# Seven buffers for the retention states, and norm sums on VectorE for three of four heads, in a hybrid decoder layer on one core

## The reference, cut to what matters

```python
# per sample b and head h, S is 256 x 512
o = (q * gamma) @ S + (q @ k) * v           # L = 1: scores, state read
S_new = gamma * S + outer(k, v)             # new_state_ret_sample
...
omu = jnp.mean(o, -1, keepdims=True)        # over the 512 columns of a head
ovar = jnp.mean(jnp.square(o - omu), -1, keepdims=True)
on = ((o - omu) * lax.rsqrt(ovar + EPS)).reshape(B, T, D_V) * ret_gn_g
y_b = (on * silu(g_ret)) @ w_ret_out
```

## Time and profile before

| | us |
|---|---|
| median of 3 runs | 788.26 |
| lowest and highest run | 786.79, 789.68 |
| the profiled execution | 790.2 |
| its span, first to last instruction | 788.3 |
| TensorE busy in it (share) | 762.3 (97%) |
| VectorE | 667.8 (85%) |
| ScalarE | 512.8 (65%) |
| mean granted clock of TensorE | 0.996 of 2.4 GHz |

### The profile page before, as it was taken

How to read it: one execution, slowest core, us unless ns; L and a number is a source line. 1 busy time by engine, 2 the same in 40 slices (tenths; PEclk the granted TensorE clock), 3 DMA queues, 4 the chain that set the end, 5 groups by cost and what they waited for, 6 DMA issues and landing times.

```text
span 788.3 us, 12126 instructions
## 1 busy us (share of the span) xinstructions
PE 762.3 (97%) x4747; PEld 655.4 (83%) x4747; DVE 667.8 (85%) x903; ACT 512.8 (65%) x641; POOL 97.3 (12%) x120
## 2 busy tenths in 40 slices
PE   9999999999998999999999998999999999999994
PEld 5999999767776789999899975888888888888873
DVE  5699999877877889899977677999888998999897
ACT  7433446566759576335586463788888788887863
POOL 1100000233332300000002001111111111110000
PEclk9999999999999999999999999999999999999998
DMA  9954454699889845454449653999999999999971
GB/s 347 385 170 178 163 189 158 213 322 335 284 291 313 296 161 180 153 197 174 160 160 334 242 214 115 354 361 370 368 379 364 362 358 368 366 367 363 345 286 75
DMA packets 39174, 213.28 MB, mean 271 GB/s; under 512 B 7381, under 2 KB 7637, under 8 KB 19244
## 3 DMA queue, kind: packets, MB, share of 16 engines
q1 hardware_dynamic: 23268, 165.39, 56.6%
q0 software_dynamic: 15408, 45.71, 16.6%
q10 hardware_dynamic: 432, 1.31, 0.4%
HBM read 193.45 MB, written 31.65 MB: 286 GB/s over the span
## 4 chain that ended last, share of the span: by engine, by line
PE 69%; DVE 13%; DMA 9%; ACT 4%; issue 2%; POOL 1%; DVEq 0%; ACTq 0%; POOLq 0%
PE bank L1868 34%; PE bank L1596 26%; DMA out_ret_sample<-S_ring 4%; DVE conv L1142 3%; DVE w_lo L1095 3%; DMA S_ring<-in_state_ret 2%; PE bank L1741 2%; PE bank L1858 2%; DMA raw<-weights 1%; DMA out_ret_sample<-S_five 1%; ACT w_hi L755 1%; PE bank L1898 1%; PE bank L1654 1%; DMA con<-constants 1%; PE bank L1613 1%
## 5 line engine op out<-in xcount | busy, mean ns | idle before, releaser
L1596 PE MATMUL bank<-h_hi,w_hi 128*128 128x264 f32 (+1 forms) x640 | 188.6, 295 | 4.3 <-DVE w_lo L1095 3.3
L1596 PE MATMUL bank<-h_lo,w_hi 128*128 128x264 f32 (+1 forms) x640 | 184.0, 288 | 0.0
L1596 PE MATMUL bank<-h_hi,w_lo 128*128 128x264 f32 (+1 forms) x640 | 184.0, 287 | 0.0
L1100 DVE TENSOR_TENSOR ring_lo<-raw,ring_hi 128x2048 fp32r<-128x2048 f32 x72 | 163.6, 2289 | 23.4 <-ACT ring_hi L762 23.4
L1095 DVE TENSOR_TENSOR w_lo<-raw,w_hi 128x1024 fp32r<-128x1024 f32 x112 | 136.8, 1222 | 32.4 <-ACT w_hi L755 31.9
L755 ACT ACTIVATE w_hi<-raw 128x1024 fp32r<-128x1024 f32 x112 | 117.8, 1052 | 56.4 <-PE bank L1596 52.4
L762 ACT ACTIVATE ring_hi<-raw 128x2048 fp32r<-128x2048 f32 x72 | 138.3, 1921 | 19.7 <-PE bank L1868 19.7
L1596 PEld LDWEIGHTS bank<-h_hi,w_hi 128*128 128x128 f32 x640 | 120.4, 188 | 10.3 <-DVE w_lo L1095 5.0
L1596 PEld LDWEIGHTS bank<-h_lo,w_hi 128*128 128x128 f32 x640 | 120.4, 188 | 0.5 <-issue 0.2
L1596 PEld LDWEIGHTS bank<-h_hi,w_lo 128*128 128x128 f32 x640 | 120.2, 188 | 0.0
L1142 DVE SCALAR_TENSOR_TENSOR conv<-u,vec,conv 128x256 f32<-128x256 f32 x240 | 101.9, 480 | 0.6
(11 more groups left out here) (291 smaller groups left out, 1491.8 us busy)
## 6 DMA issues: line engine op xcount, KB each, us to landing
raw<-weights SPq DMA_DIRECT2D x152, 1024.0 KB, 7.0
S_ring<-in_state_ret POOLq DMA_DIRECT2D x26, 512.0 KB, 7.2
out_ret_sample<-S_ring POOLq DMA_DIRECT2D x26, 512.0 KB, 6.8
S_five<-in_state_ret POOLq DMA_DIRECT2D x6, 512.0 KB, 4.8
out_ret_sample<-S_five POOLq DMA_DIRECT2D x6, 512.0 KB, 7.7
out_ret_prompt<-S_out POOLq DMA_DIRECT2D x8, 256.0 KB, 4.7
y_rows<-xg POOLq DMA_DIRECT2D x4, 512.0 KB, 7.9
raw<-y_rows SPq DMA_DIRECT2D x2, 1024.0 KB, 5.8
```

The lines of the kernel that those rows point to most:

```text
L1100: dve.tensor_tensor(ring_view(ring_lo, k), raw[raw_slot(NCM + k)][:, :].rearrange("p (k n) -> p k n", k=4), ring_view(ring_hi, k).bitcast( ...
L1596: ins = pe.matmul(out, a[:, k, cols], b[:, k0 + k, :], start=first and k == 0 and j == 0, stop=last and k == ks - 1 and j == 2)
```

## The change

There are seven slots. The two new ones (S_more) lie in xT, and xT is loaded behind the last use of them, after the last prompt state's store and before the store of the convolution's last rows. Loads of states 4, 5 and 6 are issued behind rot_ready; later the load of state n + 6 stands where that of n + 4 stood.

For heads 0 to 2 VectorE adds the four blocks of oT to one (two additions, of 528 and 264 columns, in gsq) at the end of steps 6, 10 and 14, and the four blocks of gsq at the end of steps 8, 12 and 16; TensorE multiplies only the one block. Means of heads 0 to 3 are at steps 7, 11, 15, 18 and variances at 9, 13, 17, 19, with the work of all engines that belongs to them. Head 3 keeps its steps and its groups of four.

```diff
-SLOTS = 5
+SLOTS = 7
+GM_AT, GV_AT, GM_SUM, GV_SUM = (7, 11, 15, 18), (9, 13, 17, 19), (6, 10, 14), (8, 12, 16)
...
+        S_more = xT[:, :, :].rearrange("p k n -> p (k n)")[:, 0:4 * DV].rearrange("p (s a e) -> p s a e", s=2, a=2)
...
-            return S_five if n % SLOTS == 4 else S_ring[:, n % SLOTS]
+            i = n % SLOTS
+            return S_ring[:, i] if i < 4 else S_five if i == 4 else S_more[:, i - 5]
...
             for n in range(4):
                 load(n)
-            pool.dma_start(xT[:, :, :], L["tokens_t"]).then_inc(xT_in, 16)
             pool.wait_ge(rot_ready, 8)
-            load(4)
+            for n in range(4, SLOTS):
+                load(n)
...
             store_prompt(NH - 1)
+            for i in (5, 6):
+                pool.wait_ge(S_stored[i], 16 * len(range(i, 32, SLOTS)))
+            pool.wait_ge(S_used, 32)
+            pool.dma_start(xT[:, :, :], L["tokens_t"]).then_inc(xT_in, 16)
...
-            def halved(src):
-
-                n = KT
+            def halved(dst, src, n):
+
                 while n > 1:
                     n //= 2
-                    ins = dve.tensor_tensor(ln_sq[:, 0:n, OUT], src[:, 0:n, OUT], src[:, n:2 * n, OUT], ALU.add)
-                    src = ln_sq
+                    ins = dve.tensor_tensor(dst[:, 0:n, OUT], src[:, 0:n, OUT], src[:, n:2 * n, OUT], ALU.add)
+                    src = dst
                     if n > 1:
                         link(ins)
-                ins.then_inc(csum_ready, 1)
+                return ins
...
+                    if k in GM_SUM:
+                        h = GM_SUM.index(k)
+                        evacuated(dve, ("ot", h))
+                        halved(gsq, oT[:, 4 * h:4 * h + 4, :], 4).then_inc(gsum_ready, 1)
+                    if k in GV_SUM:
+                        dve.wait_ge(osq_ready, GV_SUM.index(k) + 1)
+                        halved(gsq, gsq, 4).then_inc(gsum_ready, 1)
...
-                    if k >= 6 and (k - 6) % 4 == 0 and k <= 18:
-                        h = (k - 6) // 4
-                        evacuated(pe, ("ot", h))
-                        b = opened(("gm", h))
-                        for et in range(4):
-                            ins = pe.matmul(b[:, OUT], cst("mean_v"), oT[:, 4 * h + et, OUT], start=et == 0, stop=et == 3)
-                        done(ins)
...
+                    if k in GM_AT:
+                        h = GM_AT.index(k)
+                        if h < NH - 1:
+                            pe.wait_ge(gsum_ready, 2 * h + 1)
+                            b = opened(("gm", h))
+                            done(pe.matmul(b[:, OUT], cst("mean_v"), gsq[:, 0, OUT], start=True, stop=True))
+                        else:
+                            evacuated(pe, ("ot", h))
+                            b = opened(("gm", h))
+                            for et in range(4):
+                                ins = pe.matmul(b[:, OUT], cst("mean_v"), oT[:, 4 * h + et, OUT], start=et == 0, stop=et == 3)
+                            done(ins)
```

More of the change, by code:

```diff
@@ L255, in _tiles @@
                 add((("ot", (k - 5) // 4), "A"))
-            if k >= 6 and (k - 6) % 4 == 0 and k <= 18:
-                add((("gm", (k - 6) // 4), "D"))
-            if k >= 7 and (k - 7) % 4 == 0 and k <= 19:
-                add((("gv", (k - 7) // 4), "A"))
+            if k in GM_AT:
+                add((("gm", GM_AT.index(k)), "D"))
+            if k in GV_AT:
+                add((("gv", GV_AT.index(k)), "A"))
             if k in (20, 21):
@@ L934, in _ @@
                         act.activation(gsq[:, :, OUT], oT[:, 4 * h:4 * h + 4, OUT], ACT.Square).then_inc(osq_ready, 1)
-                    if k >= 7 and (k - 7) % 4 == 0 and k <= 19:
-                        h = (k - 7) // 4
+                    if k in GV_AT:
+                        h = GV_AT.index(k)
                         seen(act, ("gv", h))
@@ L1764, in _ @@
                         done(ins)
-                    if k >= 6 and (k - 6) % 4 == 0 and k <= 18:
-                        h = (k - 6) // 4
-                        evacuated(pe, ("ot", h))
-                        b = opened(("gm", h))
-                        for et in range(4):
-                            ins = pe.matmul(b[:, OUT], cst("mean_v"), oT[:, 4 * h + et, OUT], start=et == 0, stop=et == 3)
-                        done(ins)
[L1772 to L1776, removed]
-                            ins = pe.matmul(b[:, OUT], cst("mean_v"), gsq[:, et, OUT], start=et == 0, stop=et == 3)
-                        done(ins)
+                    if k in GM_AT:
+                        h = GM_AT.index(k)
+                        if h < NH - 1:
[8 more added lines that the diff above has]
+                            done(ins)
+                    if k in GV_AT:
+                        h = GV_AT.index(k)
+                        if h < NH - 1:
+                            pe.wait_ge(gsum_ready, 2 * h + 2)
+                            b = opened(("gv", h))
+                            done(pe.matmul(b[:, OUT], cst("mean_v"), gsq[:, 0, OUT], start=True, stop=True))
+                        else:
+                            pe.wait_ge(osq_ready, h + 1)
+                            b = opened(("gv", h))
+                            for et in range(4):
+                                ins = pe.matmul(b[:, OUT], cst("mean_v"), gsq[:, et, OUT], start=et == 0, stop=et == 3)
+                            done(ins)
                     if k in (20, 21):
```

6 lines of the change are left out of this document (3 added, 3 removed).

## The result

| | before | after |
|---|---|---|
| median of 7 runs | 789.39 (786.79 to 790.66) | 793.88 (791.12 to 795.65) |
| profiled execution: time, span, mean granted clock | 790.2, 788.3, 0.996 | 793.88, 792.1, 0.987 |

The ratio is 1.0052 (95% interval 1.0034 to 1.0069): the change makes the kernel slower, by about 4.1 us by the ratio (the two medians stand 4.5 apart). The forecast was 788.6, the range ended at 793.0.

The account below looks back on a forecast made before the run. It took TensorE's own work plus 4.5 us of idle as the bound; 8.0 + 4.2 = 12.2 off and 12.5 of new idle on gave +0.3 on 788.26, so 788.6 us, with a range of 780.5 to 793.0.

Parts of the forecast that it names:

- Part 1: Mean and variance products of heads 0 to 2 on TensorE: six four-part products become one-part, 8.0 us off.
- Parts 2 and 3: VectorE's added sums (6.9 us of work) and the later mean and variance steps: together 12.5 us of new TensorE idle.
- The chains: Queues of VectorE and ScalarE work followed through steps 8 to 19, giving 12.5 us of new TensorE idle.
- part 4: Seven state slots instead of five: ScalarE's waits for state loads vanish where they cost, 4.2 us off, bounds 0 and 4.5.
- Slower by the loads: Rival: more loads in flight each land later, ScalarE still waits in steps 11 and 15; 793 us, chance 0.20.
- The full gain: Rival: the new lags do not form, 776.1 us; chance 0.35 together with its half form at 782.4.
- The longer table switch: Rival: ScalarE held 1.3 us more behind each of three table loads, steps 9, 13, 17; 792.5 us, chance 0.01.
- Late sums: Rival: one-part products wait for additions held up by ot's copy, steps 6, 10, 14; 3 us on, 791.6, chance 0.06.

Follow-up runs that it names:

- early21: The changed kernel with means, variances and sums of heads 0 to 2 one step earlier and head 3's variance at step 21: 783.36 us (0.9925).
- shift_only: The kernel before with seven slots and the later mean and variance steps, all still in four products, no sums on VectorE: 790.78 us (1.0021).
- delay: The kernel before with seven slots, plus five unread VectorE reductions ahead of v_two in step 12: 793.7 us in a single execution.
- filled: The changed kernel with three unread 512-column products ahead of TensorE's waits in each of steps 12 and 19: 792.72 us (1.0035).
- filled_all: The changed kernel with unread 512-column products ahead of TensorE's waits in steps 11, 12, 15, 17 and 19: 791.72 us (1.0026).
- after_again: The changed kernel with nothing altered, profiled a second time: 793.2 us.
- slots7: The kernel before with only the seven slots and the later xT load, the norm as before: 787.3 us (0.9964).
- early: The changed kernel with sums one step earlier, so means of heads 0 to 2 at their old steps and their variances one later than before: 785.09 us (0.9927).
- conv_moved: The changed kernel without VectorE's convolution steps in steps 10, 11 and 14, made up for later: 797.26 us (1.0094).
- norm_only: The changed kernel with five slots and xT fetched at the start again: 800.05 us (1.0121).

## Why the prediction was wrong

- **Part 1 held.** One-part products made a step 1.34 (a product gone and one in its place) or 1.69 (gone) shorter: 6.92 to 5.58 in step 6 of early21, 6.92 to 5.22 in step 6 of after. 8.0 in all.
- **Parts 2 and 3 held in their mechanism; that the sum agrees is luck.** The chains gave 12.5 of new idle and the table has 12.5, but the steps miss by +0.3, -0.6, +0.4, -0.8 and +0.4, the 0.3 of steps 10, 14 and 18 were not forecast, and 0.3 of step 19 is clock. The largest error was step 17 (2.7 for 1.9), where the links on ScalarE were sized by likeness. shift_only divides the 12.5: the later steps alone cause 4.0. The other 8.5, more than the 8.0 that the shorter products win, come with the sums and the shorter products together; no run has the one without the other.
- **The first step that failed is a sentence at the start: "The granted clock is 1.00 there ... so clock plays no part."** It is a statement about a kernel with 4.5 of idle time, and the sum put 12.5 in its place. No price was set on idle time beyond its own length. In the profile of after the falls behind steps 12 and 19 cost 1.45 + 1.27 = 2.7. delay makes a fall with idle time, filled and filled_all take the falls away by filling it. Single profiles could do so by chance, as after_again has one fall less by itself, but the executions agree: the mean granted clock is 0.9894 over the seven of after, 0.9932 over the ten of filled_all, 0.9916 over fifty of before.
- **The second step that failed is the 4.2 of part 4, with the base that it was taken off.** ScalarE's waits did go, and the profile that the 4.2 was read from lost 4.35 by late loads. But two more profiles of before lost 2.5 and 3.3 by them, each with a fall of the clock behind one, and with no fall on either side the slots win 1.8 (slots7). The prediction saw that its profiled execution took 790.2 and the median execution 788.26, set the 1.9 between them aside as a shift of the whole, and took the waits of the slow one off the time of the quick one.
- **How much each is worth.** By the executions with a mean clock of 0.996, so with no fall on either side, before stands at 787.95, slots7 at 786.14 and filled_all, which is after with its idle filled, at 790.06: 1.8 won by the slots (forecast 4.2) and 3.9 lost by the norm's part (forecast 12.5 - 8.0 = 4.5), together +2.1 for the forecast's +0.3. The means of all executions (789.5 of before, 793.5 of after) stand 4.0 apart, so the other 1.9 go with the clock, which is lower in after's. Roughly half of the excess is part 4 and half the clock. It is rough: the fillers overshoot by some 0.4, and the levels are means of six, two and four executions.
- **The base was low.** The first three runs had a median of 788.26, seven have 789.39: 1.1 of the 5.3 by which 788.6 missed 793.88. That is noise of the measurement, not a step of the prediction.
- What is left: why the clock falls in one execution and not in the next is open, and with it why before's median execution has about two falls.
- **The rivals.** Slower by the loads named nearly the right time (793) with the wrong mechanism: ScalarE waits 1.1 for loads, not 1.7 at each of ten. The full gain stood against chains that held. The longer table switch did not show: in the profile of after each root starts 1.29 after the start of its table load, with nothing held ahead of the load. Late sums showed up nowhere: none of the one-part products waited in after.
- The marks that the prediction had set (two records, loads near 0, idle in steps 11, 12, 15, 17 and 19, "under 6 too high") were all met, with 11.9 in those five. Still the time was off, since none of them would have shown the clock or what the loads cost in other executions.

## What to carry to other kernels

Price new idle time of TensorE twice: its length, and the chance that the clock falls behind it, 1.2 to 1.6 us each in the state steps here. When work is taken off the bound engine by giving it to the one behind it, follow the second engine's queue step by step, and then move the steps until its work stands under the long ones: one step's difference turned +0.5% into -0.7% (early). And take what a late transfer costs from more than one profile: if the profiled execution is slower than the median at a higher granted clock, its waits are not those of the median one.

## What the runs showed of the hardware

**The same idle lowers the clock in some executions and not in others.** At unit 87 (step 50), behind the state steps, every kernel but conv_moved has the same wait before the layer norm's variance product, 1.33 to 1.36, in a step of 5.67:

```profile
381.62 0.71 PE L1795 MATMUL bank<-ln_sq,con 128*128 128x264 f32 x2 [1.35 <-DVE ln_sq L1120]
382.76 0.39 PE L1602 MATMUL bank<-h_hi,w_hi 128*128 128x264 f32 x1 [0.42 <-DVE w_lo L1101]
```

```profile
382.00:384.00 2.00, 1.58 (x10) 1.24 (x9) 2.00 (x3) 0.00 (x0) 0.00 (x0) 0.87 0.00 0
384.00:386.00 2.00, 2.00 (x11) 2.00 (x11) 2.00 (x4) 0.19 (x1) 0.00 (x0) 0.50 0.40 78
386.00:388.00 2.00, 2.00 (x15) 2.00 (x15) 1.85 (x2) 2.00 (x3) 0.00 (x0) 0.78 0.93 381
```

These are of slots7. The clock fell there in 5 of 13 profiles (slots7, after_again, filled_all, early, norm_only) and stayed at 1.00 in the other eight, with the start of the unit 0.02 apart in one pair (381.19 in shift_only without, 381.21 in filled_all with a fall). So a fall has a chance, not a threshold, as far as these runs can tell. The Trainium skill, TensorE: Matmul & The Clock Gate, What's actually happening, says that the window of the chip's activity monitor is free-running and does not reset when a kernel starts. That the same wait at the same time has a fall in 5 of 13 profiles agrees with it; no run here shows the monitor itself.

**A fall has no fixed price either.** It cost 1.2 to 1.6 behind steps 4, 8, 12, 17 and 19, but 3.1 in step 15 of conv_moved, where three slices in a row stood at 0.50.

**A wait for VectorE can be the length of one transfer.** The 2.12 at before's step 12 that the timeline puts down to v_two began with ScalarE's wait of 2.11 for a state load. That load took 9.7 from issue to landing there, 7.5 and 7.6 in the two other profiles, where step 12 took 11.22 and 11.54 instead of 13.26. What made it take longer is not shown.
